# Large token group first in a feed-forward stage, its operands begun earlier, and additions ahead of weight sums

## What is computed

```python
x = layer_norm(ALPHA * x + jnp.einsum('btm,md->btd', mix, w_out), ln1_g, ln1_b)
hid = jax.nn.silu(jnp.einsum('btd,df->btf', x, wg)) * jnp.einsum('btd,df->btf', x, wu)
return layer_norm(ALPHA * x + jnp.einsum('btf,fd->btd', hid, wd), ln2_g, ln2_b)
```

## Time and profile before

| | |
|---|---|
| median of 3 runs | 3255.43 us (3255.09 to 3258.55) |
| profiled execution | 3261.73 us, its span 3259.9 us |
| PE busy | 2958.3 us (91%), DVE 2221.5 (68%), ACT 1238.8 (38%), POOL 1706.5 (52%) |
| mean granted TensorE clock | 0.948 |
| feed-forward stages | from about 746 to 1640 us (layer 0) and 2362 to 3260 us (layer 1) |

### The profile page before, as it was taken

One profiled execution on the slowest core, in us unless ns is written; L12 is line 12 of the kernel. 1 busy time (PEld: TensorE's weight loads), 2 busy tenths in 40 slices (PEclk: granted clock), 3 DMA queues, 4 the chain that ended last, 5 costly groups with the idle time before them and its releaser, 6 DMA issues. The chain is left out here.

```text
span 3259.9 us, 58492 instructions
## 1 busy us (share of the span) xinstructions
PE 2958.3 (91%) x20464; PEld 2683.6 (82%) x20464; DVE 2221.5 (68%) x3913; ACT 1238.8 (38%) x2390; POOL 1706.5 (52%) x1352
## 2 busy tenths in 40 slices
PE   7979998996999989999889799989969998999997
PEld 6956666876999989999889566668769998999996
DVE  6756766647777876666654577766487778666666
ACT  3333444433444433333233244444244444333331
POOL 2323333425788766666522233434268887666665
PEclk9989997997999999999989799989989999999998
DMA  4321115533222222222232211165232222222222
GB/s 164 121 80 50 46 31 164 176 115 115 94 100 93 83 78 78 77 77 77 111 111 100 73 40 48 30 195 175 100 111 97 97 97 84 72 78 79 78 66 79
DMA packets 175526, 304.81 MB, mean 94 GB/s; under 512 B 56048, under 2 KB 97264, under 8 KB 175056
## 3 DMA queue, kind: packets, MB, share of 16 engines
q1 hardware_dynamic: 164800, 271.70, 25.8%
q0 software_dynamic: 10576, 31.14, 2.5%
HBM read 248.34 MB, written 50.38 MB: 92 GB/s over the span
## 5 line engine op out<-in xcount | busy, mean ns | idle before, releaser
L2730 PE MATMUL PS<-xoh,woph 128*128 128x256 f32 (+1 forms) x2464 | 738.4, 300 | 6.0 <-issue 6.0
L2731 PE MATMUL PS<-xol,woph 128*128 128x256 f32 (+1 forms) x2464 | 737.6, 299 | 0.0
L2732 PE MATMUL PS<-xoh,wopl 128*128 128x256 f32 (+1 forms) x2464 | 736.7, 299 | 0.0
L1470 POOL TENSOR_TENSOR wopl<-T,woph 128x512 fp32r<-128x512 f32 x348 | 505.1, 1466 | 191.3 <-ACT woph L1912 191.3
L2730 PE MATMUL PS<-hidh,wdh 128*128 128x256 f32 (+1 forms) x1408 | 428.5, 304 | 74.1 <-DVE acc L2618 52.7
L2730 PEld LDWEIGHTS PS<-xoh,woph 128*128 128x128 f32 x2464 | 468.9, 190 | 7.1 <-issue 6.8
L2732 PEld LDWEIGHTS PS<-xoh,wopl 128*128 128x128 f32 x2464 | 468.8, 190 | 0.0
L2731 PEld LDWEIGHTS PS<-xol,woph 128*128 128x128 f32 x2464 | 468.7, 190 | 0.0
L1417 POOL TENSOR_TENSOR Pl<-Pf,Ph 128x256 fp32r<-128x256 f32 (+5 forms) x174 | 218.9, 1265 | 391.8 <-DVE Ph L2297 391.8
L1912 ACT ACTIVATE woph<-T 128x512 fp32r<-128x512 f32 x348 | 217.9, 630 | 539.2 <-PE PS L2732 408.9
L2731 PE MATMUL PS<-hidl,wdh 128*128 128x256 f32 (+1 forms) x1408 | 421.3, 299 | 0.0
(11 more groups left out here) (470 smaller groups left out, 6716.5 us busy)
## 6 DMA issues: line engine op xcount, KB each, us to landing
ru<-in_W_FF SPq DMA_DIRECT2D x88, 512.0 KB, 4.1
rd<-in_W_FF SPq DMA_DIRECT2D x176, 256.0 KB, 2.8
rg<-in_W_FF SPq DMA_DIRECT2D x86, 512.0 KB, 4.0
sqt_scratch<-sqTs POOLq DMA_DIRECT2D x18, 512.0 KB, 4.2
hc<-out_H SPq DMA_DIRECT2D x18, 512.0 KB, 3.8
out_H<-yo POOLq DMA_DIRECT2D x18, 512.0 KB, 3.0
dkraw<-in_CKVT SPq DMA_DIRECT2D x16, 520.0 KB, 4.6
QS<-sqt_scratch SPq DMA_DIRECT2D x16, 512.0 KB, 3.5
```

The lines of the kernel that those rows point to most:

```text
L1470: pool.tensor_tensor(wopl[k][:, :, :], w_whole(w, k, first), f(woph[k][:, :, :]), ALU.subtract)\
L2730: pe.matmul(out, wh, mh, start=start, stop=False)
L2731: pe.matmul(out, wh, ml, start=False, stop=False)
L2732: return pe.matmul(out, wl, mh, start=False, stop=stop)
```

## The change

The groups swap sizes. Group 0 is tiles 0 to 4 and 9 (656 tokens), group 1 tiles 5 to 8 (512). x_load(0) loads five tiles. TensorE turns tiles 0 to 3 as before, then tile 4 in two banks of four blocks (x_T4), and in the middle of w_out(9) the meta rows straight from `hc` (x_T9), so that their store and reload fall away. ScalarE scales tiles 0 to 4 into `acc0` (x_in, x_in4), VectorE the meta rows in two small operations (x_in9). The order in which ScalarE makes the high parts changes, and the low parts of operands 0, 1 and 5 (A11, A12, A22) go from VectorE to GpSimd (POOL's x_op_lo), in both groups. The late tiles are turned in steps 8 to 13 of turn 0 (x_T_late) and scaled by ScalarE (x_in_late). Products 4 and 5 of turn 0 use the next two banks. The second turn's gate weights go to first_rg1 as well, so the first hid_hi waits until GpSimd has read them. In VectorE's turn product_sum and the down_adds stand before the w_sums. The last transposes wait by the new tile order, and the two w_in_lo of VectorE are put one behind last_stats(8) and one behind last_stats(9). Memory addresses follow the sizes.

```diff
-G_TOKENS = (4 * P, TOK - 4 * P)
+G_TOKENS = (5 * P + META, 4 * P)
-X_STEPS = (0, 0, 0, 1, 1, 1, 2, 2, 3, 3, 4, 4, 5, 5, 6, 6)
+X_STEPS = (8, 9, 9, 10, 10, 11, 12, 13)
-X_BY_DVE = (("lo0", "lo1", "S1", "S2", "S4", "lo2", "lo3", "S3", "lo4", "lo5", "lo6"),
-            ("lo0", "lo1", "S1", "S2", "S3", "lo2", "lo3", "lo4", "lo5", "part", "S4", "lo6"))
+X_BY_ACT = ((0, 1, 5, 3, 2, 6, 4), (0, 1, 2, 3, 4, 5, 6))
+X_BY_POOL = (0, 1, 5)
+X_BY_DVE = (("g9", "x9", "S1", "S2", "S4", "lo2", "lo3", "S3", "lo4", "lo6"),
+            ("S1", "S2", "S3", "lo2", "lo3", "lo4", "part", "S4", "lo6"))
-X_GROUPS = ((0, 1, 2, 3), (4, 5, 6, 7), (8, 9))
+X_GROUPS = ((0, 1, 2, 3, 4), (5, 6, 7, 8))
...
SP:
                 x_load(0)
                 mix_load(9)
-                first_norm_store(8)
-                residual_load(9)
+                sp.wait_ge(S("c_mixn"), A(l, TILES))
+                w_load(rg[0], 0, 0, "f_g_in")
+                sp.wait_ge(S("c_hT"), XT(l, "tiles", KD - 1) + 1)
+                w_load(first_rg1, PAIRS, 0, "f_g_in")
+                residual_load(9)
...
                 sp.wait_ge(S("f_lo"), PRODUCTS * TURNS * l + 7)
-                sp.wait_ge(S("c_hT"), XT(l, 1, 0) + 1)
-                x_load(2)
                 w_load(rg[0], 1, 0, "f_g_in")
-                sp.wait_ge(S("c_hT"), XT(l, 2, KD - 1) + 1)
-                w_load(rg[1], 1 + PAIRS, 0, "f_g_in")
+                w_load(first_rg1, 1 + PAIRS, 0, "f_g_in")
...
POOL:
                 first_root(8)
+                x_op_lo(0, 0)
+                x_op_lo(0, 1)
                 for i in range(4):
                     w_lo(0, c, i, True)
-                first_root(9)
+                x_op_lo(0, 5)
                 for i in range(4, 7):
                     w_lo(0, c, i, True)
+                first_root(9)
...
+                        if no == PAIRS - 1 and i == 9:
+                            x_op_lo(1, 0)
+                        if no == PAIRS - 1 and i == 11:
+                            x_op_lo(1, 1)
+                        if no == PAIRS - 1 and i == 13:
+                            x_op_lo(1, 5)
-                        if i == 9:
+                        if i == (13 if no == 0 else 9):
                             down_lo(j, c, 0)
...
ACT:
-                    if not first:
+                    if first:
+                        act.wait_ge(S("f_lo"), Q(j, c, PRODUCTS, 21))
+                    else:
                         act.wait_ge(S("f_down"), Q(j, c, DOWNS, 0))
                     for h in (1, 0):
...
+                        if first:
+                            for k in range(KD):
+                                if X_STEPS[k] == i:
+                                    x_in_late(k)
-                        if i == 9:
+                        if i == (13 if first else 9):
                             down_hi(j, c, 0, first)
...
                 c = TURNS * l
+                x_op_hi(0, 0)
+                x_op_hi(0, 1)
+                x_in4(0)
+                x_in4(1)
                 w_hi(0, c, 0, True)
-                x_op_hi(0, 0)
                 w_hi(0, c, 1, True)
-                x_op_hi(0, 1)
+                x_op_hi(0, 5)
+                x_op_hi(0, 3)
                 x_op_hi(0, 2)
...
DVE, turn:
                         if no == PAIRS and i == 0:
-                            x_op_lo(1, 4)
-                            x_op_lo(1, 5)
+                            x_sum_late()
+                        if i % 7:
+                            product_sum(j, c, g, i, first)
+                        if no == PAIRS and i == 1:
+                            x_op_lo(1, 6)
+                        for u in range(DOWNS):
+                            if DOWN_STEPS[u] == i and not first:
+                                down_add(j - 1, c, before, u, scaled)
                         if i == 1:
                             w_sum(j, c, 1, 1)
                             w_sum(j, c, 1, 2)
-                        if i % 7:
-                            product_sum(j, c, g, i)
-                        if no == PAIRS and i == 1:
-                            x_sum_late()
-                        if no == PAIRS and i == 2:
-                            x_op_lo(1, 6)
                         if i in (3, 4):
                             w_sum(j, c, 1, i)
                         if i == 8 and not last:
...
-                        for u in range(DOWNS):
-                            if DOWN_STEPS[u] == i and not first:
-                                down_add(j - 1, c, before, u, scaled)
-                        if first:
-                            for n in range(2 * KD):
-                                if X_STEPS[n] == i:
-                                    x_in(1 + n // KD, n % KD)
                         if first and i == 1:
                             first_norm(9)
-                        if no == PAIRS - 1 and i in (9, 10):
-                            x_op_lo(1, i - 9)
-                        if no == PAIRS - 1 and i == 11:
+                        if no == PAIRS - 1 and i == 10:
                             x_sum(1, 3)
                             x_sum(1, 2)
-                        if no == PAIRS - 1 and i == 12:
+                        if no == PAIRS - 1 and i == 11:
                             x_sum(1, 4)
                             x_op_lo(1, 2)
-                        if no == PAIRS - 1 and i == 13:
-                            x_op_lo(1, 3)
+                        if no == PAIRS - 1 and i in (12, 13):
+                            x_op_lo(1, i - 9)
                 c = TURNS * l
-                x_op_lo(0, 0)
-                x_op_lo(0, 1)
+                x_in9()
...
PE:
                 for k in range(4, KD):
-                    x_T(0, k)
-                w_out(9, 0, KD)
+                    x_T(k)
+                x_T4(0)
+                x_T4(1)
+                w_out(9, 0, 4)
+                x_T9()
+                w_out(9, 4, KD)
...
                         if first:
-                            for n in range(2 * KD):
-                                if X_STEPS[n] == i:
-                                    x_T(1 + n // KD, n % KD)
+                            for k in range(KD):
+                                if X_STEPS[k] == i:
+                                    x_T_late(k)
...
DVE, end of layer:
-                    if l + 1 < L and t == TILES - 1:
-                        w_in_lo(dve, l + 1, W_ORDER[1][KD - W_LATE])
-                        w_in_lo(dve, l + 1, W_ORDER[1][KD - W_LATE + 1])
+                    if l + 1 < L and t >= TILES - 2:
+                        w_in_lo(dve, l + 1, W_ORDER[1][KD - W_LATE + t - (TILES - 2)])
```

More of the change, by code:

```diff
@@ L540, in program @@
         early_at = m.at
-        woph = [m(f"woph{i}", [P, 4, P], F32R) if a == 0 else m(f"wopl{i}", [P, 4, P], F32R) for i in range(5) for a in range(2)]
+        woph = [m(f"woph{i}", [P, 4, P], F32R) if a == 0 else m(f"wopl{i}", [P, 4, P], F32R) for i in range(4) for a in range(2)]
         woph, wopl = woph[0::2], woph[1::2]
         assert m.at <= 139712
-        xin.append(Map(126912)("xin3", [P, D]))
+        xin += [Map(early_at + 4 * D * i)(f"xin{3 + i}", [P, D]) for i in range(2)]
         m = Map(139712)
         hid_at = m.at
-        hidh = m("hidh", [P, 2, G_TOKENS[1]], F32R)
-        hidl = m("hidl", [P, 2, G_TOKENS[1]], F32R)
-        sums_u = [m(f"sum_u{i}", [P, HALF_G[1]]) for i in range(3)]
-        upper = m("upper", [P, HALF_G[1]])
-        gate = m("gate", [P, 2, G_TOKENS[1]])
+        hidh = m("hidh", [P, 2, G_TOKENS[0]], F32R)
+        hidl = m("hidl", [P, 2, G_TOKENS[0]], F32R)
+        sums_u = [m(f"sum_u{i}", [P, HALF_G[0]]) for i in range(3)]
+        upper = m("upper", [P, HALF_G[0]])
+        gate = m("gate", [P, 2, G_TOKENS[0]])
         wd_at = m.at
@@ L563, in program @@
         acc1 = m("acc1", [P, KD, G_TOKENS[1]])
+        late_ops.insert(0, (m("woph4", [P, 4, P], F32R), m("wopl4", [P, 4, P], F32R)))
+        woph += [hi for hi, _ in late_ops]
+        wopl += [lo for _, lo in late_ops]
+        m.at = win_at + (KD + W_LATE) * 4 * INW - 4 * 4 * P - 640
         rd1 = m("rd1", [P, 4, P])
@@ L1896, in _, with w_hi @@
                     x_in(k)
-                def w_hi(j, c, i, first=False):
+                def w_hi(j, c, i, first=False, second=False):
                     w, k = i // 7, i % 7
@@ L2455, in first_norm, with x_in9 @@
                                       ALU.subtract, ALU.mult).then_inc(S("ln_out"), 1)
-                def x_in(g, k):
-                    dve.wait_ge(S("c_hT"), XT(l, g, k) + 1)
-                    out = acc1[:, k, x_cols(g).start - G_TOKENS[0]:x_cols(g).stop - G_TOKENS[0]]
-                    dve.tensor_scalar(out, x_bank(g, k), ln1T[:, 0, k:k + 1], ln1T[:, 1, k:k + 1], ALU.mult, ALU.add)\
-                       .then_inc(S("c_x1"), 1)
+                def x_in9():
+                    g9, b9 = (ln1T[:, a, :].rearrange("p (k n) -> p k n", n=1).to_broadcast([P, KD, META]) for a in range(2))
```

(30 more changed lines are left out.)

206 lines of the change are left out of this document (115 added, 91 removed).

## The result

The median of the changed kernel is 3183.9 us (3181.1 to 3186.1, 4 runs), that of the kernel before, run beside it, 3255.3 us (4 runs). The ratio is 0.9778, its 95% interval 0.9761 to 0.9795: 71 us faster. I had predicted 3184.0. The sum behind that number was right in its parts much less than in its total: the start came out some 6 us a layer worse than predicted, the turns some 7 us better, the ends some 2 us better.

A forecast was written before the change was run, and what follows sets the result against it. TensorE, busy 91%, was taken as the bound, held up by waits for VectorE and low clock. 2 x (9.3 + 2.3 + 22.1) + 3.9 = 71.3 us saved takes 3255.4 to 3184, range 3158 to 3222.

The forecast's parts named there:

- the start: Each layer's feed-forward start, up to turn 1: turn 1 begins at 790.0 instead of 799.3, 9.3 us earlier (bounds 784, 798).
- the turns: Turn 1 to last turn, each layer: waits and low clock fall from 38.6 to 16.5 us, 22.1 saved; group order 2.3.
- the ends: Ends of both layers: 1.9 us in layer 0, 2.0 in layer 1, together 3.9 us saved.
- Rivals 1 and 3: 1: VectorE and GpSimd exclude each other in narrow turns, 3209, chance 0.23; 3: GpSimd falls behind, wopl waits, 3276, 0.05.
- Rival 4: Nothing moves: turns' waits reappear at next additions, transition keeps its own, start ends 1 us later; 3249, chance 0.03.
- rival 2: Less hindrance than taken: start 785, transition 8.3, the rest 3.5; 43.1 us a layer, 3165, chance 0.09.
- The order of groups: Feed-forward turns: ten wide, one mixed, then ten narrow take 749.0 against 751.3 us bare, 2.3 us saved a layer.
- Additions before w_sums: Steady turns: waits of 1.00 (narrow) and 0.43 us (wide) go, leaving 0.2 a narrow turn and nothing a wide one.
- The prediction's own check: Bare turns, turn 11, 32.7 us of waits and 5.9 of low clock summed to 789.9, against 791.1 in the profile.
- Turn 1: First down product's wait for hidl, behind GpSimd's last w_lo: 1.0 us for 3.19 now (bounds 0 and 3.2).
- Between the groups: Transition between token groups: fewer, smaller VectorE operations cut waits from 16.5 to 11.0 us (bounds 8.3 and 16.5).
- a rival for the steady turns: Narrow turns: strict exclusion of VectorE and GpSimd keeps half their wait; 21.2 us a layer, 3209, chance 0.23.

## Why the prediction was right, and where its sum was not

**The main mechanism** was right. TensorE's waits for VectorE's queue were the cost; putting the additions first removes them in every steady turn, and nothing grows in their place: not one wait between 802 and 1192 us. Rivals 1 and 3 fall with that: their waits, in narrow turns or for wopl in the steady turns, do not exist. Rival 4, which left 3249, falls with the 71 us; rival 2, less hindrance at the start, met more of it.

**The order of groups, 2.3 us a layer.** With the measured matmul starts (39.75 / 264 = 0.1506 and 31.07 / 264 = 0.1177), turn 11 falls from 36.6 to 34.2, so 2.4. Right by arithmetic on measured turns; not run alone.

**Additions before w_sums: mis-sized.** Turns 2 to 9 and 12 to 20 lost 11.2 and 6.3 us in layer 0, 17.5 together; for these turns the prediction had 8 x 0.8 + 9 x 0.43 = 10.3 (its ninth narrow turn is turn 1). Two steps failed: that a bare turn is the turn less the wait shown (it is 0.3 us shorter still), and the 0.2 us left in each narrow turn (measured 0). The prediction's own check (its terms add up to 789.5, not 789.9, against 791.1 us) could not catch that: it puts back the same waits that it had taken off to get the bare turns.

**Turn 1.** 1.0 us of wait was predicted and 0.31 measured. From its first down product to that of turn 2, turn 1 took 35.1 us before, 4.0 more than a bare narrow turn, and takes 39.8 now, 0.1 more than a bare wide one; the granted clock from 801 to 806 us is 1.00. With the wait that is 2.9 + 3.9 = 6.8 us less. The prediction had 2.2 for the wait, 0.8 for the steady wait and, for the clock here and between the groups together, 5.9 - 2.5 = 3.4. Right in kind and a little small: the low clock that it still expected here did not come.

**Between the groups.** 11.0 us of waits predicted; measured 9.3 in layer 0 and 10.8 in layer 1, against 16.5. These are the rows of layer 0, TensorE's timeline of the changed kernel:

```profile
1192.29 0.64 PE L2780 MATMUL PS<-hidh,wdh 128*128 128x328 f32 x1 [2.55 <-DVE acc L2679]
...
1198.64 0.42 PE L2780 MATMUL PS<-hidh,wdh 128*128 128x328 f32 x1 [1.91 <-DVE acc L2679]
...
1207.99 0.39 PE L2780 MATMUL PS<-hidh,wdh 128*128 128x328 f32 x1 [2.40 <-DVE hidl L2626]
...
1216.85 0.42 PE L2780 MATMUL PS<-hidh,wdh 128*128 128x328 f32 x1 [2.46 <-DVE acc L2679]
```

The size was nearly right and the reason only in part: I gave 6 us of it to fewer and smaller operations of VectorE, GpSimd's three among them, but with those back on VectorE this stretch is within 1.5 us of the same. Nor does the new order of additions shorten the longest wait: with it alone, the 7.87 us are 8.35.

**The start, 9.3 us: wrong.** The first down product came 3.9 and 4.3 us earlier from mix_T, where about 10 was predicted. Turn 1 itself, reckoned back from it as the prediction does (801.09 - 0.31 - 36 x 0.1506 = 795.4), begins 4.1 us earlier on the clock and, with the 1.9 us by which this profile is ahead at mix_T, only 2.2 us earlier for the 9.3. The step that failed is "VectorE then has 8 operations [...] it enters turn 0 at 765.4", which counts small ones as free and names no first_norm(8): that alone took 8.87 us. TensorE's x_T9 behind it ended at 744.7 where 742.5 was predicted, the last projection, at half clock for 5 us, at 752.0 where 748 was, and VectorE entered turn 0 at 769.1; with the 1.9 us these are 746.6, 753.9 and 771.0. The hindrance that the earlier trace rows show cost more here too, at 758.3, where a weight sum of 0.69 us took 3.47 beside GpSimd's x_op_lo(0, 5), as VectorE's and then GpSimd's timeline show:

```profile
758.32 3.47 DVE L2621 TENSOR_TENSOR T<-first_rg 128x512 f32<-128x512 f32 x1
```

```profile
756.98 4.26 POOL L1499 TENSOR_TENSOR xol<-acc,xoh 128x1312 fp32r<-128x1312 f32 x1
```

That weight sum is what product 4 waited 5.59 us for. Moving the three operands was counted as relief; it is a loss of about 5 us a layer at this place, though a 1312-column operand took GpSimd 3.0 us when nothing hindered it, not the 3.3 of the prediction. The Trainium skill, page SBUF — State Buffer, section Who interferes with whom, would not have made it relief. At this place the runs side with the rule and not with the durations by which the prediction went; it had weighed the rule as a rival for the steady turns, where no wait came of it. The rows of the two weight sums, which have two inputs, agree with it (3.32 and 3.47 us); that a VectorE instruction stands behind four in a row it does not say.

**Ends, 3.9 us: an omission.** The last stretch of the table shrank by 4.2 us and not 2.0. The last turn's 96 down matmuls come after y_T began, and they are now narrow: 96 x (0.152 - 0.119) = 3.2 us a layer, which the prediction left out. With the 2.0 that would be 5.2, a little more than was measured. That this is the rest is worked out, not tried.

The three misses, +6 us a layer at the start, -7 in the turns and -2 at the ends, nearly cancel; what they leave is less than the 9 us by which the two profiled executions lie further apart than the medians. The median agreed to 0.1 us by luck; the range, 3158 to 3222, is what the working had earned.

## What to carry to other kernels

A wait shown in front of a pipelined matmul costs more than it shows, and after one of 5.4 us the granted clock was 0.52 for 5 us more: take the difference of the starts of matmuls, or of whole turns, and not the idle time. On an engine that several others wait for, first do what TensorE needs next and only then what has slack; that alone was half or more of this gain. Before work is moved from VectorE to GpSimd, look at what VectorE must do at that very moment: GpSimd's instructions without a gap can hold a short VectorE instruction for their whole run, and here leaving the work on VectorE was faster.

## What the runs showed of the hardware

A VectorE instruction of 0.80 us took 8.80 to 9.38 us, until four GpSimd instructions in a row had ended, in six kernels, in two forms, over 16 and over 128 partitions, while VectorE's sums of two tensors, and the same operation on another tile, got in after one. A matmul shown as 0.28 us long starts 0.12 us after the one before, and the first step after a wait is 0.22 us. After TensorE's wait of 5.41 us the granted clock was 0.52 for 5 us; in the kernel without that wait it stayed at 1.00 there.
